# Cutting the attention scores of a hybrid layer into products of 64 by 64

## The chip, the cores and the metric

The kernel runs on one core of a Trainium2 chip. The metric is the device time of one execution in microseconds; lower is better. Times of a run are given as a median; a profile is one execution in which every instruction is recorded. The engines are TensorE (PE; its weight loads, LDWEIGHTS, have a row of their own, PEld), VectorE (DVE), ScalarE (ACT), GpSimd (POOL) and SyncE (SP), which here only issues transfers.

## The reference

Two blocks are computed one after the other on 512 tokens of width 2048 in float32. The first is one hybrid layer: a dilated banded attention of 16 heads of 64 features (three window and dilation settings, joined by a softmax over their log denominators), a gated linear recurrence of 8 heads, an output projection and a gate. The second is two layers, each with a retention of 6 heads, a differential attention of 4 heads (each with two score maps of 64 features) and a gated recurrence. Cut to what matters here:

```python
# first block: 16 heads, E = 64
q = rope_partial(heads(aq, 16), pos) * (64 ** -0.5)
k = rope_partial(heads(ak, 16), pos)
s = einsum('bdhnqe,bdhnke->bdhnqk', qb, kb)        # scores: contraction over 64 features
s = where(valid, s, NEG)                           # banded, dilated windows
pe = exp(s - max(s)); o = einsum(pe, vb) / sum(pe)

# second block, per layer: 4 heads x 2 maps, DQ = 64, causal
s = einsum('bqhcd,bkhcd->bhcqk', qb, k)            # blocks of 128 queries
p = softmax(where(kpos <= qpos, s, -inf))
w = p[:, :, 0] - lam * p[:, :, 1]
o = einsum('bhqk,bkhe->bqhe', w, v)
```

The rest of both blocks is projections with 2048 inputs, norms, gates, the recurrences and the output projections.

## The kernel before, in words

The kernel is written engine by engine: each engine has its own program, and semaphores order them. A wait stands in an engine's queue, and all behind it on this engine waits too. Most of TensorE's work is the projections. A tile of 128 output features is 16 blocks of 128 inputs; both operands are split into a high and a low float32r part, so a block is three matmuls of 128 by 128 weights on 512 tokens (`quarter`, L325). A quarter is 4 blocks, 12 matmuls, and `step` runs 4 tiles of 4 quarters, p = 0 to 15. ScalarE copies the high part of the weights (`high`, L710), GpSimd subtracts to get the low part (L262), both paced by `w_free`, which each quarter raises.

After quarter p, `step` runs the attention or recurrence work that belongs to this p, for heads whose projections ended a step earlier. For the first attention (`att_work`) a step takes a pair of heads, 8 pairs in all. Queries and keys of head 0 lie on partitions 0 to 63, those of head 1 on 64 to 127. `att_scores` (L468 to L475) makes the scores of one block of 128 queries against 512 keys for both heads, as one float32 matmul each, weights of 64 rows by 128 queries; a float32 matmul is two instructions in the trace. Head 0 goes to PSUM bank SC[0], head 1 to SC[1]. Blocks 0 to 3 stand at p = 0, 4, 8, 12. Ahead of each product stands a wait for `sm_done`: VectorE has read the scores that the bank held before (L1434, which also finds the row maximum). ScalarE then takes the exponential, VectorE scales and transposes, and `att_values` (L487, 32 by 64 weights) runs for the pair before at p = 0, right behind block 0's scores. Pair 0 is a step of its own, pairs 1 to 6 are a loop. The last pair has no tiles of its own to run with: `step(None, ...)` puts the blocks at p = 0, 2, 6, 10 (`LAST_PAIR`), with the first output projection tiles (`pair_step`, L358) between, and its values at p = 15.

The second attention (`dif_work`) is built alike: `dif_scores` (L551 to L558) for block a multiplies only the first 128 (a + 1) keys, because it is causal, at p = 0, 4, 8, 12 of a step (`GROUPED`), with waits for `dsm_done` (VectorE's read, L1523). Two layers have 4 heads each, all inside steps with tiles. Around its scores stand transposes (L389, L576) and values (L567) with weights of 128 by 128. The retention steps hold a gate product (L547) whose weights are 128 rows by 32 or 64 columns on 512 tokens.

The order on each engine is written out by hand; no planner moves anything.

Of the kernel before, what the change touches and what calls it, by code (L numbers as in the profile page):

```python
# [31 lines left out]
P = 128  # L32
# [8 lines left out]
PRIMED = 1  # L41
# [41 lines left out]
def lru_features(s):  # L83

    if s < X_JOIN:
# [8 lines left out]
GROUPED = dict(scores={0: 0, 4: 1, 8: 2, 12: 3}, softmax={1: 0, 5: 1, 9: 2, 13: 3}, turn={4: 0, 8: 1, 12: 2},  # L94
               values={8: 0, 12: 1}, turn_late={0: 3}, values_late={0: 2, 4: 3}, last=4, back=6, out=5, dif_out=6, v_copy=4)

ATT_POINTS = dict(scores={0: 0, 4: 1, 8: 2, 12: 3}, softmax={1: 0, 5: 1, 9: 2, 13: 3})
LAST_PAIR = dict(scores={0: 0, 2: 1, 6: 2, 10: 3}, softmax={1: 0, 4: 1, 8: 2, 12: 3})
# [28 lines left out]
def build(nc, wt, xT, pT, pos1, pos2, par1, par2, dlam, gw, cst, idn, masks, bias, dec, cmask, out):  # L127
    ctx = ExitStack()
    with ctx:  # L129
# [5 lines left out]
        def sem(name):  # L135
            if name not in sems:
                sems[name] = ctx.enter_context(nc.semaphore(name))
            return sems[name]
# [28 lines left out]
        SC = [ctx.enter_context(nc.psum_tensor(f"scores{i}", [P, S], F32)) for i in range(2)]  # L167
# [4 lines left out]
        def row(r, n=1):  # L172
            return W[:, r, :] if n == 1 else W[:, r:r + n, :]
# [22 lines left out]
        QT, KTR, VTA, QN, KN, RW, TM = 22, 23, 24, 25, 26, 27, 28  # L196
# [112 lines left out]
        def _(pe):  # L309
            def quarter(t, q, gen=None, spare=None, behind=2):  # L310

                bank = Z[t.odd] if spare is None else spare
                if q == 0 and spare is None:
                    if t.c in (T_HGG, T_HGG + 1) and not t.terms:
                        pe.wait_ge(sem("e_out"), 16)
                    else:
                        pe.wait_ge(sem("z_free"), t.times(1, 1 - T_HGG - behind))
                pe.wait_ge(sem("l_ready"), t.times(4, q + 1))  # L320
                for k in range(4 * q, 4 * q + 4):
                    if gen is not None:
                        pe.wait_ge(sem("u_ready"), gen * 16 + k + 1)
                    for n, (w, u) in enumerate(((WH, UH), (WH, UL), (WL, UH))):
                        mm = pe.matmul(bank[:], w[:, k, :], u[:, k, :], start=(k == 0 and n == 0),  # L325
                                       stop=(k == KT - 1 and n == 2))
                mm.then_inc(sem("w_free"), 1)
# [137 lines left out]
                if p == 14:  # L465
                    turn_v(row(HTMP), (sem("ho_scaled"), j + 1), "ho_turned", TP[1])

            def att_scores(j, a):  # L468

                for hd in range(2):  # L470
                    u = 2 * a + hd
                    pe.wait_ge(sem("sm_done"), PRIMED + j * 8 + max(u - 1, 0))
                    o = 64 * hd
                    pe.matmul(SC[hd][:], row(QT)[o:o + 64, a * P:(a + 1) * P], row(KTR)[o:o + 64, :],
                              start=True, stop=True).then_inc(sem("s_done"), 1)  # L475

            def att_values(j):

                pe.wait_ge(sem("vx_ready"), j * 16 + 16)
                pe.wait_ge(sem("p_ready"), PRIMED + j * 8 + 8)  # L480
                pe.wait_ge(sem("att_done"), PRIMED + j)
                for kb in range(16):
                    k = slice(32 * kb, 32 * kb + 32)
                    for g in range(4):
                        rows = slice(32 * g, 32 * g + 32)
                        for hd in range(2):
                            mm = pe.matmul(ATT_BANKS[g][64 * hd:64 * hd + 64, 0:P].rearrange("p (a t) -> p a t", a=4),  # L487
                                           VX[rows, hd, kb, :], W[rows, PTB + 4 * hd:PTB + 4 * hd + 4, k],
                                           start=(kb == 0), stop=(kb == 15))
                mm.then_inc(sem("av_done"), 1)  # L490

            def att_work(j, p, late=None, at=ATT_POINTS):

                if p == 0:
                    pe.wait_ge(sem("qt_ready"), j + 1)
                if p in at["scores"]:
                    att_scores(j, at["scores"][p])
                if late is not None and p == 0:
                    att_values(late)
                if p == 15 and at is LAST_PAIR:  # L500
                    att_values(j)
# [49 lines left out]
            def dif_scores(j, a):  # L551

                for hd in range(2):
                    u = 2 * a + hd
                    pe.wait_ge(sem("dsm_done"), PRIMED + j * 8 + max(u - 1, 0))
                    o, w = 64 * hd, (a + 1) * P
                    pe.matmul(SC[hd][:, 0:w], row(QT)[o:o + 64, a * P:(a + 1) * P], row(KTR)[o:o + 64, 0:w],
                              start=True, stop=True).then_inc(sem("ds_done"), 1)  # L558

            def dif_values(j, a):  # L560

# [21 lines left out]
            def dif_work(j, p, late=None):  # L583

                at = GROUPED
                if p == 0:
                    turn_v(row(VTA), (sem("dqt_ready"), j + 1), "dv_turned", VB)
                if p in at["scores"]:
                    dif_scores(j, at["scores"][p])
                if late is not None and p in at["values_late"]:  # L590
                    dif_values(late, at["values_late"][p])
                if p in at["values"]:
                    dif_values(j, at["values"][p])
                if late is not None and p in at["turn_late"]:
                    dif_turn(late, at["turn_late"][p])
                if p in at["turn"]:
                    dif_turn(j, at["turn"][p])
                if late is not None and p == at["back"]:
                    dif_turn_back(late)

            WORK = {"hg": hg_work, "att": att_work, "ret": ret_work, "dif": dif_work}

            def step(t, work=None, j=None, between={}, behind=(2, 2, 2, 2), **kw):

                for p in range(16):
                    s, q = divmod(p, 4)
                    if t is not None:
                        quarter(t.plus(s), q, behind=behind[s])
                    if work is not None:
                        WORK[work](j, p, **kw)  # L610
                    if p in between:
                        between[p]()

            pe.wait_ge(sem("p_split"), 2)
            for m in range(KT):
                t, n = divmod(m, 8)
# [4 lines left out]
                for k in range(2):  # L621
                    for i, (w, u) in enumerate(((WH, PH), (WH, PL), (WL, PH))):
                        mm = pe.matmul(Z[m % 2][:], w[:, 2 * n + k, :], u[:, k, :], start=(k == 0 and i == 0),
                                       stop=(k == 1 and i == 2))
                mm.then_inc(sem("w_free") if n % 2 else sem("e_even"), 1)

            for m in range(8):
                for q in range(4):
                    quarter(Tile(T_HGG + m), q, 0 if m == 0 else None, SPARE.get(m), 4 if m in (4, 5) else 2)
                if m == 2:  # L630
                    pe.wait_ge(sem("consts"), 16)
                    pe.wait_ge(sem("ones_set"), 1)
                    sum_rows(row(ACC), OB, (sem("sq_used"), PRIMED + 16), "ss_done")
            step(Tile(T_HG))
            with pe.Fori(1, HG_HEADS) as i:
                step(Tile(T_HG, (4, i)), work="hg", j=i - 1)
            step(Tile(T_ATT), work="hg", j=HG_HEADS - 1)
            step(Tile(T_ATT + 4), work="att", j=0, between={7: lambda: pe.wait_ge(sem("hg_done"), PRIMED + HG_HEADS)})
            with pe.Fori(2, PAIRS) as i:
# [20 lines left out]
            for l in range(LAYERS):  # L660
# [7 lines left out]
                for h in range(1, RET_HEADS + 1):  # L668
                    if h == 1:
# [4 lines left out]
                         j=l * RET_HEADS + h - 1, b=h - 1)  # L674
# [3 lines left out]
                with pe.Fori(2, DIF_HEADS) as i:  # L678
                    step(Tile(T_L2 + R_DIF, (PER_LAYER, l), (4, i)),
                         work="dif", j=l * DIF_HEADS + i - 1, late=l * DIF_HEADS + i - 2)  # L680
# [1354 lines left out]
```

## Time and profile before

| what | value |
|---|---|
| median of 3 runs | 3036.71 us (3035.82 to 3039.58) |
| the profiled execution | 3036.43 us, its span 3034.6 us |
| TensorE busy | 2955.4 us, 97% |
| VectorE, GpSimd, ScalarE busy | 1649.8, 1315.0, 1284.9 us |
| granted TensorE clock, mean | 0.991 |

The span runs from the first to the last instruction. An engine's busy time counts an instant once, however many of its instructions overlap. Matmuls overlap their neighbours in the record, so the distance between starts tells more of their cost than their durations.

### The profile page before, as it was taken

What the parts mean: (1) busy time and instruction counts of PE and PEld (TensorE: products, weight loads), DVE (VectorE), ACT (ScalarE), POOL (GpSimd) and SP (SyncE); (2) the same over time, 40 slices, a digit from 0 to 9 for tenths busy, and PEclk for the clock granted to TensorE, in tenths of its full rate; (3) what the DMA queues carried; (4) which work ended last, traced back from release to release, by engine and by line L of the source; (5) the groups of instructions that cost most, each with busy time, mean ns of one, the idle gap of its engine ahead of it and who ended that gap; (6) DMA issues with size and microseconds to landing.
All of it is one profiled execution on the core that took longest, in us unless ns stands there. A gap on an engine that the chain in (4) does not pass through costs nothing.

```text
span 3034.6 us, 48369 instructions
## 1 busy us (share of the span) xinstructions
PE 2955.4 (97%) x17162; PEld 2385.6 (79%) x17162; DVE 1649.8 (54%) x2349; ACT 1284.9 (42%) x2468; POOL 1315.0 (43%) x1002
## 2 busy tenths in 40 slices
PE   8999999999999999989999999999999999999997
PEld 6888888877777787767887878788778878787886
DVE  5367666655656315657565664561275656654412
ACT  6545444354556333443333333453343333344432
POOL 4444444443433343553444444344444444444444
PEclk9999999999999999999999999999999999999999
DMA  6223222222222323233222222232242222222322
GB/s 238 102 90 111 83 83 76 77 84 83 78 77 80 125 97 139 90 118 125 105 87 91 87 85 82 83 142 100 104 156 88 95 87 96 84 84 80 143 97 97
DMA packets 60880, 305.72 MB, mean 101 GB/s; under 512 B 5712, under 2 KB 6096, under 8 KB 29776
## 3 DMA queue, kind: packets, MB, share of 16 engines
q1 hardware_dynamic: 38224, 259.54, 24.0%
q10 hardware_dynamic: 22528, 44.50, 4.2%
q8 instruction: 77, 1.26, 0.2%
q14 instruction: 51, 0.42, 0.0%
HBM read 285.67 MB, written 18.35 MB: 100 GB/s over the span
## 4 chain that ended last, share of the span: by engine, by line
issue 56%; POOL 32%; PE 9%; POOLq 1%; DMA 1%; ACT 1%; DVE 0%; DVEq 0%; ACTq 0%; SPq 0%
POOL w_low L262 31%; PE z L325 8%; DMA w_raw<-in_wt 1%; POOLq L261 1%; POOL next_weights L270 0%; PE scores L325 0%; PE v_bank L358 0%; PE z L358 0%; ACT u_high L722 0%; DVE mixed L1647 0%; POOLq L296 0%; DVE work L1266 0%; POOLq L284 0%; POOLq L129 0%; ACT w_high L710 0%
## 5 line engine op out<-in xcount | busy, mean ns | idle before, releaser
L262 POOL TENSOR_TENSOR w_low<-w_raw,w_high 128x512 fp32r<-128x512 f32 x932 | 1254.3, 1350 | 1700.0 <-ACT w_high L710 1692.5
L325 PE MATMUL z<-u_high,w_high 128*128 128x512 f32 x3408 | 1347.6, 395 | 2.6 <-POOL w_low L262 1.8
L325 PE MATMUL z<-u_high,w_low 128*128 128x512 f32 x3408 | 1328.4, 390 | 0.0
L325 PE MATMUL z<-u_low,w_high 128*128 128x512 f32 x3408 | 1327.0, 389 | 0.0
L710 ACT ACTIVATE w_high<-w_raw 128x512 fp32r<-128x512 f32 x928 | 578.7, 628 | 1223.0 <-PE z L325 1128.3
L325 PEld LDWEIGHTS z<-u_high,w_high 128*128 128x128 f32 x3408 | 640.1, 188 | 160.2 <-issue 23.3
L325 PEld LDWEIGHTS z<-u_high,w_low 128*128 128x128 f32 x3408 | 639.6, 188 | 136.1
L325 PEld LDWEIGHTS z<-u_low,w_high 128*128 128x128 f32 x3408 | 640.5, 188 | 127.1
L1633 DVE TENSOR_TENSOR work<-work 128x512 f32<-128x512 f32 x87 | 99.9, 1148 | 365.0 <-ACT work L947 351.7
L1260 DVE TENSOR_TENSOR work<-z,work 128x512 f32<-128x512 f32 x110 | 76.1, 692 | 122.7 <-PE z L325 101.8
L1292 DVE SCALAR_TENSOR_TENSOR work<-z,work 32x512 f32<-32x512 f32 (+1 forms) x176 | 120.9, 687 | 2.4
L735 ACT ACTIVATE work<-work 128x512 f32<-128x512 f32 x72 | 45.4, 631 | 145.4 <-DVE work L1272 92.1
L341 PE MATMUL z<-u_high,next_weights 128*128 128x512 f32 x192 | 72.1, 417 | 21.1 <-DVE u_low L1618 13.6
L722 ACT ACTIVATE values_spread<-work 32x512 f32<-32x512 f32 x128 | 80.6, 630 | 19.4 <-DVE work L1449 16.4
L1316 DVE TENSOR_TENSOR work<-o_bank,head_norm 128x512 f32<-128x512 f32 x28 | 19.4, 692 | 112.5 <-ACT head_norm L748 112.5
L1279 DVE TENSOR_TENSOR mixed<-work 128x512 f32<-128x512 f32 (+1 forms) x35 | 24.3, 694 | 85.4 <-ACT work L739 85.4
L1288 DVE SCALAR_TENSOR_TENSOR work<-z,work 128x512 f32<-128x512 f32 x56 | 38.7, 692 | 58.7 <-PE z L325 56.7
L1296 DVE TENSOR_TENSOR work<-work 128x512 f32<-128x512 f32 x56 | 65.4, 1168 | 5.2
L341 PEld LDWEIGHTS z<-u_high,next_weights 128*128 128x128 f32 x192 | 38.5, 200 | 35.5 <-issue 23.4
L1347 DVE TENSOR_TENSOR work<-work 128x512 f32<-128x512 f32 x56 | 55.0, 983 | 18.8 <-ACT work L722 10.8
L722 ACT ACTIVATE work<-work 128x512 f32<-128x512 f32 (+1 forms) x96 | 58.3, 639 | 13.9 <-DVE work L1347 9.7
L1474 DVE SCALAR_TENSOR_TENSOR work<-work 128x512 f32<-128x512 f32 x72 | 60.8, 845 | 6.0 <-issue 0.9
(281 smaller groups left out, 3243.7 us busy)
## 6 DMA issues: line engine op xcount, KB each, us to landing
w_raw<-in_wt SPq DMA_DIRECT2D x241, 1024.0 KB, 4.8
out_hT<-work ACTq DMA_DIRECT2D x8, 1024.0 KB, 8.7
work<-out_hT ACTq DMA_DIRECT2D x8, 1024.0 KB, 10.4
work<-in_xT SPq DMA_DIRECT2D x4, 1024.0 KB, 17.2
e_scratch<-work ACTq DMA_DIRECT2D x1, 4096.0 KB, 16.7
work<-in_xT ACTq DMA_DIRECT2D x4, 1024.0 KB, 10.9
work<-in_dec ACTq DMA_DIRECT2D x12, 256.0 KB, 2.7
work<-rope_tables ACTq DMA_DIRECT2D x10, 256.0 KB, 2.8
```

The source lines that it names most:

```text
L262: pool.tensor_tensor(WL[:, 4 * q:4 * q + 4, :], RAW[:, t.odd, 512 * q:512 * q + 512].rearrange("p (k c) -> p k c", k=4), WH[:, 4 * q:4 * q ...
L325: mm = pe.matmul(bank[:], w[:, k, :], u[:, k, :], start=(k == 0 and n == 0), stop=(k == KT - 1 and n == 2))
L341: mm = pe.matmul(bank[:], w[x], u[:, k, :], start=(k == 0 and n == 0), stop=(k == KT - 1 and n == 2))
L710: act.activation(WH[:, 4 * q:4 * q + 4, :], RAW[:, n.odd, 512 * q:512 * q + 512].rearrange("p (k c) -> p k c", k=4), ACT.Copy).then_inc(se ...
L722: i = act.activation(dst, src, ACT.Copy, **kw)
L735: act.activation(row(r), row(r), ACT.Exp, scale=-1.0)
L1260: v.tensor_tensor(dst, (Z[t.odd] if bank is None else bank)[:], row(RSTD), ALU.mult).then_inc(sem("z_free"), 1)
L1292: i = v.scalar_tensor_tensor(out=row(TM)[o:o + half], in0=z[x:x + half, :], scalar=-scale if first else scale, in1=row(sin)[o:o + half], o ...
L1296: v.tensor_tensor(row(dst), row(dst), row(TM), ALU.add)
L1347: i = v.tensor_tensor(x, x, y, ALU.mult)
L1474: v.scalar_tensor_tensor(out=R_, in0=R_, scalar=-1.0 / f, in1=TB, op0=ALU.add, op1=ALU.mult)
L1633: i = v.tensor_tensor(row(ACC), row(ACC), row(SQ0 + s), ALU.add)
```

## The change

Both score helpers now cut each head's product of 64 rows by 128 queries into two of 64 by 64: the first 64 queries go to partitions 0 to 63 of the bank, the others to 64 to 127, against the same keys. In `att_scores` a new argument `whole` keeps head 0 as one product of 64 by 128 and cuts head 1 only; it is true at p = 0 and in the last pair. The waits between the heads are gone. Where `whole` is true one wait stands ahead of both heads; elsewhere it stands ahead of the projection quarter that precedes the scores. Each wait now asks for both heads' reads of the block before. Each head still raises its semaphore once.

```diff
-            def att_scores(j, a):
-
+            def att_scores(j, a, whole):
+
+                if whole:
+                    pe.wait_ge(sem("sm_done"), PRIMED + j * 8 + 2 * a)
                 for hd in range(2):
-                    u = 2 * a + hd
-                    pe.wait_ge(sem("sm_done"), PRIMED + j * 8 + max(u - 1, 0))
-                    o = 64 * hd
-                    pe.matmul(SC[hd][:], row(QT)[o:o + 64, a * P:(a + 1) * P], row(KTR)[o:o + 64, :],
-                              start=True, stop=True).then_inc(sem("s_done"), 1)
+                    o, w = 64 * hd, P if whole and hd == 0 else 64
+                    for x in range(0, P, w):
+                        mm = pe.matmul(SC[hd][x:x + w, :], row(QT)[o:o + 64, a * P + x:a * P + x + w], row(KTR)[o:o + 64, :],
+                                       start=True, stop=True)
+                    mm.then_inc(sem("s_done"), 1)
...
-                    att_scores(j, at["scores"][p])
+                    att_scores(j, at["scores"][p], p == 0 or at is LAST_PAIR)
...
             def dif_scores(j, a):
                 for hd in range(2):
-                    u = 2 * a + hd
-                    pe.wait_ge(sem("dsm_done"), PRIMED + j * 8 + max(u - 1, 0))
-                    o, w = 64 * hd, (a + 1) * P
-                    pe.matmul(SC[hd][:, 0:w], row(QT)[o:o + 64, a * P:(a + 1) * P], row(KTR)[o:o + 64, 0:w],
-                              start=True, stop=True).then_inc(sem("ds_done"), 1)
+                    o, n = 64 * hd, (a + 1) * P
+                    for x in (0, 64):
+                        mm = pe.matmul(SC[hd][x:x + 64, 0:n], row(QT)[o:o + 64, a * P + x:a * P + x + 64],
+                                       row(KTR)[o:o + 64, 0:n], start=True, stop=True)
+                    mm.then_inc(sem("ds_done"), 1)
...
                 for p in range(16):
                     s, q = divmod(p, 4)
+                    if work == "dif" and p in GROUPED["scores"]:
+                        pe.wait_ge(sem("dsm_done"), PRIMED + j * 8 + 2 * GROUPED["scores"][p])
+                    if work == "att" and t is not None and p in (4, 8, 12):
+                        pe.wait_ge(sem("sm_done"), PRIMED + j * 8 + p // 2)
                     if t is not None:
                         quarter(t.plus(s), q, behind=behind[s])
```

## Rows read from the trace of the kernel before

**Rows 1.** The page, part 1: busy us, share of the span, instructions.
```profile
PE 2955.4 (97%) x17162; PEld 2385.6 (79%) x17162; DVE 1649.8 (54%) x2349; ACT 1284.9 (42%) x2468; POOL 1315.0 (43%) x1002
```
**Rows 2.** Busy time by stretch: length, each engine, granted clock, transfers.
```profile
590.00:955.00 365.00, 363.56 (x2992) 279.90 (x2991) 206.47 (x403) 194.81 (x359) 148.96 (x115) 1.00 0.23 81
955.00:1010.00 55.00, 45.45 (x647) 34.14 (x646) 37.48 (x79) 31.73 (x63) 8.94 (x7) 0.91 0.11 39
1780.00:2000.00 220.00, 219.83 (x1039) 175.14 (x1038) 114.63 (x218) 92.77 (x215) 93.14 (x71) 1.00 0.23 82
...
962.70:964.60 1.90, 1.90 (x4) 0.47 (x4) 1.12 (x2) 0.59 (x2) 0.00 (x0) 0.50 0.00 0
```
**Rows 3.** Groups by shape: count, busy us, mean ns, idle before and its cause.
```profile
L474 PE MATMUL scores<-work 64*128 64x512 f32 x128 | 37.7, 657 | 4.8 <-DVE work L1302 4.2 <-DVE small L1434 0.6
...
L557 PE MATMUL scores<-work 64*128 64x512 f32 x32 | 9.0, 641 | 0.0
```
**Rows 4.** Timeline (start us, us) around one first-attention site, loads and matmuls.
```profile
673.70 0.19 PEld L325 LDWEIGHTS z<-u_high,w_low 128*128 128x128 f32 x1
674.24 0.30 PEld L474 LDWEIGHTS scores<-work 64*128 64x128 f32 x4 [0.35 <-issue]
...
674.24 0.70 PE L474 MATMUL scores<-work 64*128 64x512 f32 x2
...
674.77 0.60 PE L474 MATMUL scores<-work 64*128 64x512 f32 x2
...
675.29 0.19 PEld L325 LDWEIGHTS z<-u_high,w_high 128*128 128x128 f32 x1 [0.76 <-issue]
```
**Rows 5.** Timeline of weight loads at a second-attention site of 128 keys.
```profile
1833.11 0.30 PEld L557 LDWEIGHTS scores<-work 64*128 64x128 f32 x4 [0.17 <-issue]
1833.53 0.19 PEld L567 LDWEIGHTS o_bank<-work 128*128 128x128 f32 x1
```
**Rows 6.** Timeline of weight loads at two gate products of the retention.
```profile
1510.93 0.16 PEld L547 LDWEIGHTS scores<-work 128*32 128x32 f32 x8 [0.35 <-issue]
...
1512.78 0.19 PEld L325 LDWEIGHTS z<-u_high,w_high 128*128 128x128 f32 x1 [0.84 <-issue]
...
1561.12 0.20 PEld L547 LDWEIGHTS scores<-work 128*64 128x64 f32 x4 [0.35 <-issue]
1561.60 0.14 PEld L547 LDWEIGHTS scores<-work 128*64 128x64 f32 x2 [0.29 <-issue]
1562.03 0.14 PEld L547 LDWEIGHTS scores<-work 128*64 128x64 f32 x2 [0.28 <-issue]
1562.99 0.19 PEld L325 LDWEIGHTS z<-u_high,w_high 128*128 128x128 f32 x1 [0.81 <-issue]
```
**Rows 7.** Timeline where a transpose of 128 by 128 follows a quarter.
```profile
1484.76 0.39 PE L325 MATMUL z<-u_high,w_low 128*128 128x512 f32 x1
...
1484.77 0.14 PEld L513 LDWEIGHTS turned<-identity,work 128*128 128x128 f32 x1
```
**Rows 8.** Timeline of TensorE at block 0 of a pair.
```profile
698.60 1.13 PE L474 MATMUL scores<-work 64*128 64x512 f32 x4
699.66 0.34 PE L487 MATMUL turned<-work,values_spread 32*64 32x128 f32 x4
```
**Rows 9.** Timeline of TensorE and VectorE in the last pair.
```profile
962.66 2.08 PE L474 MATMUL scores<-work 64*128 64x512 f32 x4 [4.21 <-DVE work L1302]
...
970.58 0.71 DVE L1447 STREAM_TRANSPOSE work<-work 128x512 f32<-128x512 f32 x1 [0.30 <-PE v_bank L487]
...
999.03 0.34 PE L487 MATMUL turned<-work,values_spread 32*64 32x128 f32 x4 [3.93 <-issue]
```
**Rows 10.** Timeline: VectorE's last read of a block, and the next scores.
```profile
928.82 0.69 DVE L1434 CUSTOM_DVE_ANT_0 work<-scores,work 128x512 f32<-128x512 f32 x1
...
936.74 0.70 PE L474 MATMUL scores<-work 64*128 64x512 f32 x2
...
1791.46 0.29 DVE L1523 CUSTOM_DVE_ANT_0 work<-scores,work 128x128 f32<-128x128 f32 x1
...
1795.50 0.49 PE L557 MATMUL scores<-work 64*128 64x256 f32 x2
```

## The prediction, made before the changed kernel ran

> **What bounds the kernel now.** I read the page's busy shares first, then the busy time by stretch, then the matmul groups by shape, then single sites of the two edited helpers in the timeline. TensorE is busy for 97% of the span [rows 1]. In the stretches that hold the edited helpers it is busier still: 363.6 of 365 us where the first attention runs and 219.8 of 220 us where the second does in layer 1, both at full clock; only in the 55 us around the last pair is it idle for 9.6 us [rows 2]. The groups by shape say the same: the 128 matmuls of the first attention's scores have 4.8 us of idle time before them, 4.2 behind one wait and 0.6 behind another, and those of the second have none [rows 3]. So a microsecond added to or taken from TensorE's stream in these stretches is a microsecond of the kernel, the last pair excepted. Other engines don't enter.
>
> **What one site costs now.** A site is the products of both heads for one block of 128 queries: 4 matmul instructions, since each f32 product is two. The first attention has 128 of 512 columns, so 32 sites; the second has 32 of each of four widths, so 32 sites too (the widest in [rows 3]). Within a site the heads already run side by side: two instructions start at 674.24, the other two at 674.77, and the projection's weights load at 675.29 [rows 4]. So a site is two phases, not four, and some 1.06 us from its own weight load to the next one (674.24 to 675.29; 1.06 at the site of 698.60 [rows 8]). With 128 columns it is 0.42 (1833.11 to 1833.53 [rows 5]): 384 columns less in each of two phases are worth 0.64 us, so 512 columns stream in 0.427 us and 128 in 0.107, and about 0.20 us stand around the streaming at either width.
>
> The array is full in both phases: 2 heads x 64 rows, 128 output rows. Cutting each product into two of 64 by 64 gives four products on four quarters of the array, again in two phases of the same length. **Nothing is taken from the streaming.** What can change is what stands around it.
>
> **The split sites.** The diff splits both heads where `whole` is false: 7 pairs x 3 blocks = 21 sites in the first attention and all 2 x 4 x 4 = 32 in the second, 53 in all. No row shows 64x64 on four quarters. The nearest is a gate product of 128 rows by 64 weight columns [rows 6]: two quarters, four phases of 512 columns, 1.87 us from 1561.12 to 1562.99. Two phases less, 2 x 0.427, is 1.02 us, against 1.06 with 128 weight columns: 0.04 us less, because only 64 columns are loaded before streaming begins. Its first phase says it too, 0.48 us (1561.12 to 1561.60) against 0.53 (674.24 to 674.77). From the other side, with four narrow products side by side, 128x32, it is 1.85 for four phases (1510.93 to 1512.78 [rows 6]), so four products at once cost no more. Bounds: 0 per site (twice as many instructions to issue eat the shorter load) and 0.06 (the narrow form, 1.06 - 1.00). I take 0.04, by the row of the same width: 53 x 0.04 = 2.1 us saved, bounds 0 and 3.2.
> The Trainium skill (TensorE: Matmul & The Clock Gate, LDWEIGHTS) prices a weight load by its columns over 1.2 GHz, whatever its rows, so 64 fewer are an estimate of 0.053 us a site and 2.8 us in all, within these bounds.
>
> **The mixed sites.** Where `whole` is true head 0 stays 64 by 128 and head 1 becomes two of 64 by 64: block 0 of 7 pairs, and all 4 blocks of the last pair, 11 sites. Here two cuts of the array meet inside one site. What does the trace show when the cut changes? With the same cut the weights of the next product load while the current one streams, even across a wait and another line: L513's load starts at 1484.77 under the projection's matmul of 1484.76 [rows 7]. When the cut changes the load is held back: before the scores it starts at 674.24, 0.54 us after the one before it and with 0.35 us of idle time, and after them at 675.29, when both phases are out [rows 4]. The change of rows alone does it (128x128 to 64x128, [rows 4]) and the change of columns alone too (128x128 to 128x64, idle 0.35 before the load [rows 6]). So TensorE empties before it goes on in another cut. In none of these rows are the two products on separate parts of the array, so the trace doesn't show that head 1's rows 64 to 127 must wait for head 0's rows 0 to 63. I take it that they do: the load is held even where a spare weight buffer is plainly free in the same-cut case, so what is checked seems to be the cut, not the place.
> The Trainium skill (TensorEngine Tiling (Array Packing), Key Properties) says that changing the mode, and not just the tile, drains the engine; by it the sum is the one below, and by the bare rows, which show only overlapping places, the first rival stays open.
>
> Then head 0 takes its 1.06 us and head 1 comes after it with another 1.02 (the 64-column site above): +1.02 us a site. For the 7 sites at block 0 that is 7 x 1.02 = 7.1 us, all on the path, since the next work, the late values at 699.66, starts 1.06 us after the scores of 698.60 [rows 8]. In the last pair block 0 runs after a wait of 4.21 us at a granted clock of 0.50 [rows 2, 9]; by that clock its 1.02 would be about 1.9 (streaming doubled, 2 x 0.853, and 0.2 around it). It is passed on: VectorE waits for the values that follow (0.30 us at 970.58 [rows 9]) and is then the engine that the pair's end hangs on. The other three sites of that pair add 3 x 1.02 to TensorE, but it stands still for 3.93 us before the last values at 999.03, where the softmax is late [rows 9]; they are absorbed. Sum: +7.1 + 1.9 = +9.0 us. Bounds: 0 (heads overlap as now) and 7.1 + 1.9 + 3.1 = 12.1 (nothing absorbed).
>
> **The moved waits.** The wait before block a now stands ahead of a quarter of 12 matmuls, 2.73 us (12.18 us from one site to the next, less 1.26 for the site and the held load, over four), and asks for both heads' reads of block a - 1 at once. Behind it on TensorE are the quarter and its release of weight buffers to ScalarE. The reads are done long before in the first attention: the tightest ends at 929.5, the quarter starts at about 933.9 (936.74 less 2.73 and the 0.09 before the load). In the second the tightest is block 0 of each layer's first head: read done at 1791.8, quarter at about 1792.7, so 0.9 us in hand [rows 10]. Cost 0, and at most the lateness beyond 0.9 us at two places; if VectorE came 1 us later there, 0.2 us in all. In the last pair the wait for both heads delays head 0 of block 3 from 986.33 to about 986.95, before the same 3.93 us of slack. Removing the wait between the heads frees nothing: they start together now.
>
> **Sum.** 3036.43 us for the profiled execution (span 3034.6) + 9.0 - 2.1 = 3043.3. That execution is 0.3 us below the median of 3036.71; I say 3043.4.
>
> **Rivals.**
> 1. *The mixed sites overlap as before.* Head 1's quarters are free while head 0 streams. For it: two heads do run in one phase now [rows 4]. Against it: the held loads. Then only the split sites count: 3036.4 - 2.1 = 3034.3. The Trainium skill (TensorE: Matmul & The Clock Gate, Part 3) has weight loads overlap running matmuls exactly when the row group differs, as it does here; that would give this rival.
> 2. *The 64-column halves don't run side by side* with two row halves in use. Each split site then takes twice its streaming: 21 x 0.85 = 17.9, and in the second attention 8 x (0.21 + 0.43 + 0.64 + 0.85) = 17.0; the mixed sites' second halves another 7 x 0.85 + 1.7 = 7.7. With the sum above, 3043.3 + 42.6 = 3086. Slower whatever the mixed sites do. Against it: two products of 128x64 and four of 128x32 do share a phase [rows 6], and four of 32x64 start together in the values [rows 8].
> 3. *The hoisted wait lets the scores' weights load under the quarter.* If the 0.20 us around a site were the wait's doing, 53 x 0.20 = 10.6 us would go: 3035 with the drained mixed sites, 3026 without them. Against it: L513 has a wait ahead of it and loses nothing, and the projection's load after the scores is held too [rows 4, 7].
> 4. *A later wait in the projection*, by the 0.9 us margin: under 1 us, no case of its own.
>
> **How the numbers follow.** The forecast 0.62, rival 1 0.27, rival 2 0.04, rival 3 0.05, anything else 0.02. The forecast's own range is 3041 to 3046: its +6.9 moves with the 1.9 of the half-clock site, the absorbed 3.1 and the 0 to 3.2 of the split sites. The range that holds 8 in 10 has to take in rival 1: 3033.2 to 3046. A run of this kernel can tell about 0.2%, 6.1 us, from no change. The forecast lies at +6.7 against the median, just beyond it: I give it 0.7 to end above. Slower: 0.62 x 0.7 + 0.04 + 0.01 = 0.48. Faster, from rival 3 and the unknown rest: 0.05. Same: 0.47.
>
> **What would show it.** In the changed profile: at a mixed site (block 0 of a pair) matmuls in four start times instead of two, about 2.1 us from the first load to the next work; at a split site eight instructions in two start times, first phase 0.48 us instead of 0.53, 1.02 in all; the same idle time before the scores' load; no new wait of TensorE for VectorE's reads; the 3.93 us before the last values shrunk to about 2.8. If the mixed sites take 1.06 us, the drain step is wrong and the kernel is no slower. If a split site of 512 columns takes 1.9 us, the side-by-side step is.

## The result and the profile after

The changed kernel takes 3043.89 us (median of 20 runs, 3041.32 to 3047.77) against 3036.42 us of the kernel before (20 runs, 3035.22 to 3039.58): ratio 1.0025, 95% interval 1.0019 to 1.0031. That is 7.5 us slower, a quarter of a per cent; 3043.4 was forecast. The profiled execution took 3046.1 us, its span is 3044.3 us, so it is one of the longer ones, and 9.7 us above the span of before.

The page after, part 1, answers to [rows 1]: TensorE's busy time is up by 10.4 us, the other engines' by 3.2 at most.

```profile
PE 2965.8 (97%) x17396; PEld 2381.4 (78%) x17396; DVE 1648.4 (54%) x2349; ACT 1288.1 (42%) x2468; POOL 1312.9 (43%) x1002
```

The timeline of weight loads and matmuls (start us, us) at a split site of the first attention, the same place as [rows 4]. The site's eight matmul instructions, two for each of its four products, start in two groups, four at 676.11 and four at 676.59; from the site's load to the projection's it is 1.02 us, and the load is held back by the same 0.35 us as before.

```profile
675.57 0.19 PEld L325 LDWEIGHTS z<-u_high,w_low 128*128 128x128 f32 x1
676.11 0.21 PEld L475 LDWEIGHTS scores<-work 64*64 64x64 f32 x8 [0.35 <-issue]
...
676.11 0.66 PE L475 MATMUL scores<-work 64*64 64x512 f32 x4
...
676.59 0.61 PE L475 MATMUL scores<-work 64*64 64x512 f32 x4
...
677.13 0.19 PEld L325 LDWEIGHTS z<-u_high,w_high 128*128 128x128 f32 x1 [0.81 <-issue]
```

The weight loads at block 0 of a pair, the same place as [rows 8]. Head 0's two loads come first; head 1's four wait 1.05 us for them, with 0.76 us in which no weight loads, and the late values start at 702.45, 2.06 us after the site instead of 1.06.

```profile
700.39 0.29 PEld L475 LDWEIGHTS scores<-work 64*128 64x128 f32 x2 [0.35 <-issue]
701.44 0.20 PEld L475 LDWEIGHTS scores<-work 64*64 64x64 f32 x4 [0.76 <-issue]
702.45 0.15 PEld L489 LDWEIGHTS turned<-work,values_spread 32*64 32x64 f32 x4 [0.81 <-issue]
```

Starts of the scores of pair 2 and block 1 after it, from TensorE's timeline: 12.14 us between split sites (12.18 before) and 17.00 after a mixed one with the late values behind it (15.96 before).

```profile
676.11 1.09 PE L475 MATMUL scores<-work 64*64 64x512 f32 x8
...
688.25 1.09 PE L475 MATMUL scores<-work 64*64 64x512 f32 x8
...
700.39 2.13 PE L475 MATMUL scores<-work 64*128 64x512 f32 x6
...
717.39 1.09 PE L475 MATMUL scores<-work 64*64 64x512 f32 x8
```

The groups by shape, answering to [rows 3]: neither attention's scores wait for a read of VectorE. The only wait left is the last pair's for its queries.

```profile
L475 PE MATMUL scores<-work 64*64 64x512 f32 x212 | 36.5, 632 | 0.0
L475 PE MATMUL scores<-work 64*128 64x512 f32 x22 | 13.3, 686 | 4.2 <-DVE work L1308 4.2
L558 PE MATMUL scores<-work 64*64 64x512 f32 x64 | 8.7, 614 | 0.0
```

In the last pair, TensorE's timeline, answering to [rows 9]. Block 0 takes 3.97 us at half clock. A projection tile then stands still for 1.78 us between two of its own matmuls, block 1 takes 3.02, and the last values follow the tile of 1009.04 directly: the 3.93 us of idle time ahead of them are gone (1.14 us of idle time now stand among the values, at 1012.99).

```profile
969.05 3.97 PE L475 MATMUL scores<-work 64*128 64x512 f32 x6 [4.21 <-DVE work L1308]
...
979.15 0.39 PE L358 MATMUL z<-u_low,w_high 128*128 128x512 f32 x1
981.32 0.39 PE L358 MATMUL z<-u_high,w_low 128*128 128x512 f32 x1 [1.78 <-issue]
981.63 3.02 PE L475 MATMUL scores<-work 64*128 64x512 f32 x6
...
1009.04 0.39 PE L358 MATMUL z<-u_high,w_low 128*128 128x512 f32 x1
1009.36 0.34 PE L489 MATMUL turned<-work,values_spread 32*64 32x128 f32 x4
```

The stretch after that stall, busy time by stretch with the granted clock third from the end: 0.73 of full speed, where this part of the last pair had 1.00 before (980 to 990 us). It is half clock (1.2 of 2.4 GHz) up to about 989.5 us and full clock from there.

```profile
983.00:995.00 12.00, 12.00 (x36) 6.92 (x33) 10.18 (x18) 6.43 (x12) 1.73 (x1) 0.73 0.00 0
982.70:989.40 6.70, 6.70 (x16) 4.07 (x16) 4.95 (x12) 2.94 (x7) 0.00 (x0) 0.50 0.00 0
989.60:995.00 5.40, 5.40 (x22) 2.97 (x21) 5.11 (x7) 3.53 (x6) 1.73 (x1) 1.00 0.00 0
```

Where the 9.7 us of the two profiles come from: from the first pair's block 0 to the last pair's it is 373.6 us (595.47 to 969.05) instead of 367.1 (595.58 to 962.66), +6.5; from there to the third output tile (1018.60, before 1008.44) 49.6 instead of 45.8, +3.8; the second attention's split sites give back about 1, and what is left, under 1 us, lies in the projections between.

### The profile page after: what moved, and what is told of

Same layout as the page of the kernel before. It is cut to its first block, busy times and chain, and to the rows that moved or that the text cites. A ratio compares the mean times of both kernels' runs of the same rounds, so it can differ in the third digit from the quotient of the medians.

```text
span 3044.3 us, 48808 instructions
## 1 busy us (share of the span) xinstructions
PE 2965.8 (97%) x17396; PEld 2381.4 (78%) x17396; DVE 1648.4 (54%) x2349; ACT 1288.1 (42%) x2468; POOL 1312.9 (43%) x1002
## 4 chain that ended last, share of the span: by engine, by line
issue 56%; POOL 32%; PE 9%; POOLq 1%; DMA 1%; ACT 1%; DVE 0%; DVEq 0%; ACTq 0%; SPq 0%
POOL w_low L262 31%; PE z L325 8%; DMA w_raw<-in_wt 1%; POOLq L261 1%; POOL next_weights L270 0%; PE scores L325 0%; PE v_bank L358 0%; PE z L358 0%; ACT u_high L728 0%; DVE mixed L1653 0%; POOLq L296 0%; DVE work L1272 0%; POOLq L284 0%; ACT w_high L716 0%; ACT next_weights L723 0%
## 5 line engine op out<-in xcount | busy, mean ns | idle before, releaser
L1322 DVE TENSOR_TENSOR work<-o_bank,head_norm 128x512 f32<-128x512 f32 x28 | 19.3, 691 | 113.2 <-ACT head_norm L754 113.2
```

## The experiments

All are edits of the changed kernel; "the cut" is the shape in which a product occupies the array. Theory D is the prediction's: a second cut inside a site drains TensorE, so head 1 follows head 0.

**1. No mixed sites.**

```diff
-                    o, w = 64 * hd, P if whole and hd == 0 else 64
+                    o, w = 64 * hd, P if whole else 64
```

> The mixed sites (block 0 of every pair and the last pair) get both heads as 64 by 128 again; all else as changed. Theory D (a second cut inside a site drains TensorE, so head 1 follows head 0): the 9 us of the mixed sites go and the 53 split sites keep their 0.04 us, 3036.4 - 2.1 = 3034.3 us, ratio to before 0.9993, sites at block 0 back to 1.06 us. Rival W (the time comes from the moved waits or from more instructions, not from the mix): stays above 3040 us.

Measured: 3034.93 us (11 runs), before 3036.76, ratio 0.9995 (0.9986 to 1.0004). With head 0 and head 1 in one cut everything that the change cost is gone, though its waits, its split sites and most of its added instructions are still there. Rival W falls. Sites at block 0 are 1.06 us again (15.96 us to the next). That it is faster than before isn't shown by the times, whose interval holds 1.

**2. All sites of the first attention mixed.**

```diff
-                    o, w = 64 * hd, P if whole and hd == 0 else 64
+                    o, w = 64 * hd, P if hd == 0 else 64
```

> All 32 sites of the first attention are mixed, head 0 as 64 by 128 and head 1 as two of 64 by 64. Theory D: the 21 other sites each lose the 0.04 us and pay 1.02 more, 21 x 1.06 = 22.3 us over the changed kernel's 3043.9, so 3066.2 us, and the distance between sites goes from 12.14 to 13.20 us. Rival S (only block 0, with the late values behind it, is slow when mixed): no more than the changed kernel plus 1 us, 3045.

Measured: 3063.15 us (5 runs), ratio 1.0086 (1.0072 to 1.0100). The weight loads of a block 1, with a projection quarter behind it and not the late values, show the same wait for head 0:

```profile
609.05 0.29 PEld L475 LDWEIGHTS scores<-work 64*128 64x128 f32 x2 [0.35 <-issue]
610.10 0.20 PEld L475 LDWEIGHTS scores<-work 64*64 64x64 f32 x4 [0.76 <-issue]
611.11 0.19 PEld L325 LDWEIGHTS z<-u_high,w_high 128*128 128x128 f32 x1 [0.81 <-issue]
```

The distance between sites is 13.16 to 13.17 us. That is 1.02 more than split (12.14) and 0.98 more than uncut (12.18), so 21 x 1.025 = 21.5 us against the changed kernel, where 22.3 were expected; 19.3 were measured. The rest fits the last pair, which in this profile lacks the stall of 1.78 us and takes 47.0 us instead of 49.6. Rival S (only block 0) falls by 18 us. The price of a mixed site over the kernel before is 0.98 us where a projection follows it.

**3. The waits alone.**

```diff
-                    o, w = 64 * hd, P if whole and hd == 0 else 64
+                    o, w = 64 * hd, P
...
-                    for x in (0, 64):
-                        mm = pe.matmul(SC[hd][x:x + 64, 0:n], row(QT)[o:o + 64, a * P + x:a * P + x + 64],
-                                       row(KTR)[o:o + 64, 0:n], start=True, stop=True)
+                    mm = pe.matmul(SC[hd][:, 0:n], row(QT)[o:o + 64, a * P:(a + 1) * P],
+                                   row(KTR)[o:o + 64, 0:n], start=True, stop=True)
```

> Only the waits are moved as in the change; every product is 64 by 128 as before. Theory D and the prediction's step on waits: 3036.4 us, within 0.3 us of before. Rival W (a wait ahead of the quarter holds up the projection, or lets the scores' weights load under it): slower by some us, or faster by up to 10.6 us if the 0.20 us around a site were the wait's.

Measured: 3037.01 us (11 runs), before 3036.76, ratio 1.0002 (0.9993 to 1.0011); sites 12.18 us apart, as before. So the waits cost and free nothing that the sites or the times show. The part of rival 3 that lays the 0.20 us around a site at the wait's door falls too.

**4. The last pair uncut.** Its four blocks get both heads as 64 by 128, block 0 of the others stays mixed.

```diff
-                    o, w = 64 * hd, P if whole and hd == 0 else 64
+                    o, w = 64 * hd, P if both or whole and hd == 0 else 64
...
-                    att_scores(j, at["scores"][p], p == 0 or at is LAST_PAIR)
+                    att_scores(j, at["scores"][p], p == 0 or at is LAST_PAIR, at is LAST_PAIR)
```

> The last pair's four blocks get both heads as 64 by 128; block 0 of the other 7 pairs stays mixed, the rest stays split. Theory D: 7 x 1.02 - 2.1 = +5.0 us over before, 3041.4 us; the last pair's share of the changed kernel is what is left, 3043.9 - 3041.4 = 2.5 us. Rival L (the last pair, with its half clock, makes most of the 7.5 us): below 3039 us.

Measured: 3041.38 us (11 runs, 3040.75 to 3042.39), before 3036.76, ratio 1.0015 (1.0006 to 1.0024). Over experiment 1 that is 6.45 us for 7 mixed sites, 0.92 each by the times. By the profile the distance to block 1 grows by 0.99 us in pair 0 (12.18 to 13.17) and by 1.04 in the pairs with late values behind block 0 (15.96 to 17.00), with pair 1 counted alike 7.2 us in all; each median's interval is nearly 3 us wide to either side and doesn't tell 6.45 from 7.2. Rival L (most of it in the last pair) falls: 6.5 of the 9 us by which the changed kernel lies above experiment 1 are at block 0 of the seven pairs.

**5. Narrower still: four of 64 by 32 a head,** block 0 and the last pair uncut.

```diff
-                    o, w = 64 * hd, P if whole and hd == 0 else 64
+                    o, w = 64 * hd, P if whole else 32
...
-                    for x in (0, 64):
-                        mm = pe.matmul(SC[hd][x:x + 64, 0:n], row(QT)[o:o + 64, a * P + x:a * P + x + 64],
+                    w = 32
+                    for x in range(0, P, w):
+                        mm = pe.matmul(SC[hd][x:x + w, 0:n], row(QT)[o:o + 64, a * P + x:a * P + x + w],
```

> As the kernel without mixed sites (block 0 of every pair and the last pair 64 by 128), but the 53 split sites are cut into four of 64 by 32 per head instead of two of 64 by 64. Theory D with the weight columns as the price before streaming: the distance between first-attention sites goes from 12.14 to 12.12 us, another 53 x 0.02 = 1.1 us, 3033.9 us. Rival I (16 matmul instructions a site cost issue time): 12.14 us or more, 3035 or above.

Measured: 3037.47 us (11 runs), before 3036.83, ratio 1.0001 (0.9992 to 1.0010). Sites are 12.14 us apart, as with 64 columns, and the site's own 1.02 us is unchanged:

```profile
674.65 0.18 PEld L475 LDWEIGHTS scores<-work 64*32 64x32 f32 x16 [0.35 <-issue]
675.67 0.19 PEld L325 LDWEIGHTS z<-u_high,w_high 128*128 128x128 f32 x1 [0.84 <-issue]
```

Rival I holds, and single instructions show how. In another profile of this kernel, at the site whose load starts at 675.81, the second group of matmuls starts 0.455 us after the load, against 0.482 with 64 columns and 0.535 with 128:

```profile
676.27 0.64 PE L475 MATMUL scores<-work 64*32 64x512 f32 x8
```

So the shorter load does save 0.027 us. But the instructions of a group start 7 ns apart, and the last of eight starts 0.50 us after the load, as does the last of four with 64 columns: the extra instructions take back what the shorter load gives.

The median is also 2.5 us above experiment 1's, and its interval against before doesn't tell it from nothing. The sites don't explain it. In that other profile the last pair, uncut in both, takes 47.8 us against experiment 1's 45.4, so the difference may lie there.

**6. Two cuts, neither of them 64 by 128.** In blocks 1 to 3 of the first attention head 0 is two of 64 by 64, head 1 four of 64 by 32.

```diff
-                    o, w = 64 * hd, P if whole and hd == 0 else 64
+                    o, w = 64 * hd, P if whole else (64, 32)[hd]
```

> No product of 64 by 128 at the 21 sites of blocks 1 to 3 of the first attention: head 0 is two of 64 by 64, head 1 four of 64 by 32; the rest as in the kernel without mixed sites. Theory D (any two cuts side by side drain): distance between sites 13.12 to 13.16 us, 21 x 1.0 = +21 us, 3056 us. Rival F (only an uncut row half, 64 by 128, can't run beside a cut one): 12.14 us, 3034.9 us.

Measured: 3056.67 us (4 runs), ratio 1.0065 (1.0049 to 1.0080). The distance is 13.10 to 13.11 us, and the weight loads of the two cuts are 1.01 us apart, though the two heads use different halves of the rows:

```profile
621.90 0.20 PEld L475 LDWEIGHTS scores<-work 64*64 64x64 f32 x4 [0.35 <-issue]
622.91 0.15 PEld L475 LDWEIGHTS scores<-work 64*32 64x32 f32 x8 [0.81 <-issue]
623.90 0.19 PEld L325 LDWEIGHTS z<-u_high,w_high 128*128 128x128 f32 x1 [0.84 <-issue]
```

So it isn't the uncut half that blocks (rival F): both pairs of cuts that were tried, 64 by 128 beside 64 by 64 and 64 by 64 beside 64 by 32, follow one another. In both the heads share the columns and differ in the rows; parts that differ in the columns alone weren't tried.

**7. The second attention mixed, the first not.** Head 0 is 64 by 128, head 1 two of 64 by 64, for 128 to 512 keys.

```diff
-                    o, w = 64 * hd, P if whole and hd == 0 else 64
+                    o, w = 64 * hd, P if whole else 64
...
-                    for x in (0, 64):
+                    w = (P, 64)[hd]
+                    for x in range(0, P, w):
```

> The 32 sites of the second attention are mixed (head 0 64 by 128, head 1 two of 64 by 64), those of the first are split or 64 by 128 but never mixed. Theory D says head 1's streaming is added, which grows with the keys: 2 phases x 0.427 x n/512 and some 0.13 around it, 0.34, 0.56, 0.77 and 0.98 us for 128 to 512 keys, 8 x 2.65 = 21.2 us, less nothing; 3034.9 + 21.2 + 1.3 (the 0.04 us lost at 32 sites are in it) = 3056 to 3057 us. Rival P (a fixed penalty of 0.98 us whenever the cut changes inside a site): 32 x 0.98 = 31.4 us, 3066 us.

Measured: 3058.46 us (4 runs), ratio 1.0072 (1.0057 to 1.0087). A site of 128 keys now takes 0.78 us (0.42 in [rows 5]), one of 512 keys 2.06:

```profile
1835.41 0.61 PEld L559 LDWEIGHTS scores<-work 64*128 64x128 f32 x6 [0.17 <-issue]
1836.19 0.30 PEld L570 LDWEIGHTS o_bank<-work 128*128 128x128 f32 x2 [0.17 <-issue]
...
1875.43 0.29 PEld L559 LDWEIGHTS scores<-work 64*128 64x128 f32 x2 [0.35 <-issue]
1876.49 0.20 PEld L559 LDWEIGHTS scores<-work 64*64 64x64 f32 x4 [0.76 <-issue]
1877.49 0.19 PEld L570 LDWEIGHTS o_bank<-work 128*128 128x128 f32 x1 [0.81 <-issue]
```

The distances between sites over those of the changed kernel grow by 0.40, 0.63, 0.83 and 1.04 us with 128, 256, 384 and 512 keys. The price is head 1's own streaming plus some 0.19 us, and no fixed penalty (rival P). 8 x 2.90 = 23.2 us; over experiment 1 it is 23.5.

**8. and 9. The changed kernel again, twice.**

> The changed kernel once more, for the last pair. In its first profile TensorE stood still for 1.78 us inside a projection tile at 979.5 us and ran at half clock afterwards. If that belongs to the change, it is there again and the time is 3043 to 3044 us; if it is chance, the second profile has the last pair some 2 us shorter, while the 7 sites at block 0 keep 13.16 us to the next one.

> The changed kernel a third time. Its first profile had 49.6 us from the last pair's block 0 to the third projection tile, its second 46.3, the kernel before 45.8. If the difference between the two is a stall that comes and goes (1.78 us inside a tile and the half clock after it), this profile lies anywhere between 46 and 50 us, the sites at block 0 of the other pairs show 13.16 us again, and the time is 3041.5 to 3044 us.

Measured: 3042.32 us (11 runs, 3041.73 to 3045.43, profiled 3042.14) and 3045.05 us (9 runs, 3041.69 to 3046.14, profiled 3046.14). Taken together with the first 20, 17 of 40 runs lie between 3041.3 and 3043.0 and 23 between 3043.3 and 3047.8, while experiment 4, whose last pair is uncut, has all 11 within 1.6 us. In the second profile the last pair takes 46.3 us, the stall inside the tile is 0.74 us, and the clock stays up:

```profile
981.12 0.39 PE L358 MATMUL z<-u_high,w_low 128*128 128x512 f32 x1 [0.74 <-issue]
981.44 0.69 PE L475 MATMUL scores<-work 64*128 64x512 f32 x1
```

The stretch of 983 to 995 us of the same profile, busy time by stretch with the granted clock third from the end:

```profile
983.00:995.00 12.00, 12.00 (x51) 8.04 (x48) 11.13 (x24) 9.65 (x18) 1.34 (x1) 1.00 0.00 0
```

In the third profile (first line) it is 50.2 us, the stall 1.98 and the clock 0.72 in the same 12 us. A fourth profile of the same kernel, whose span is 3044.2 us, has 49.3 us, a stall of 1.46 and 0.72 (second line):

```profile
983.00:995.00 12.00, 12.00 (x36) 7.04 (x35) 10.18 (x18) 6.05 (x12) 1.43 (x1) 0.72 0.00 0
983.00:995.00 12.00, 12.00 (x36) 7.02 (x34) 10.58 (x20) 6.46 (x13) 1.40 (x1) 0.72 0.01 1
```

The three profiles with spans of 3044.2 and 3044.3 us have the long stall and the low clock, that of 3040.3 us (3042.14 us in all) has neither. So 3 to 4 us of the changed kernel come and go with this one place; the sites at block 0 are the same in all four (13.17 us to the next in pair 0, 16.97 to 17.00 in pairs 2 to 6).

**10. Only the last pair mixed, and 11. only its blocks 1 to 3.**

```diff
-                    o, w = 64 * hd, P if whole and hd == 0 else 64
+                    o, w = 64 * hd, P if whole and (both or hd == 0) else 64
...
-                    att_scores(j, at["scores"][p], p == 0 or at is LAST_PAIR)
+                    att_scores(j, at["scores"][p], p == 0 or at is LAST_PAIR, at is not LAST_PAIR)   # 10
+                    att_scores(j, at["scores"][p], p == 0 or at is LAST_PAIR, p == 0)                # 11
```

> Only the last pair's four blocks are mixed; block 0 of the other pairs is 64 by 128 for both heads, the rest is split. Theory D with the prediction's sum for the last pair: 3034.9 (no mixed sites) + 1.9 = 3036.8 us. Rival L (the last pair costs what the first profile of the changed kernel shows, 3.8 us): 3038.7 us.

> Only blocks 1 to 3 of the last pair are mixed. Prediction's step (3 x 1.0 us more of TensorE, absorbed by its 3.93 us of idle time ahead of the last values): 3034.9 us, the idle time 3.9 - 3 = about 1 us or the wait before block 3 gone instead, values at the same distance from block 0. Rival N (nothing is absorbed): 3037.9 us.

Measured: 3036.00 us for 10 (11 runs, 3033.89 to 3039.57; ratio 1.0000, 0.9991 to 1.0009) and 3034.64 us for 11 (11 runs; ratio 0.9995, 0.9986 to 1.0004), before 3036.34. Blocks 1 to 3 cost nothing: the last pair takes 45.4 us from its block 0 to the third tile (962.35 to 1007.75), as in experiment 1. TensorE's waits there in 11: the 0.6 us ahead of block 3 is gone and the one ahead of the values shrinks from 3.9 to 2.7.

```profile
PE scores L475 <- DVE work L1308: 4.2, 1, 4.2
PE turned L489 <- issue: 2.7, 1, 2.7
```

With block 0 mixed too (10) it is 47.1 us, 1.7 more, and 1.1 to 1.4 us by the medians. Here the whole last pair is mixed, as in the changed kernel, and yet there is no stall inside a tile and TensorE still stands idle before the last values:

```profile
999.55 0.34 PE L489 MATMUL turned<-work,values_spread 32*64 32x128 f32 x4 [2.12 <-issue]
```

## Why the prediction was right

- **Nothing taken from streaming, four products side by side:** right. A split site's instructions start in two groups; rival 2 would have shown 1.9 us where 1.02 is.
- **Split sites, 0.04 us each:** right for 512, 384 and 256 keys (12.18 to 12.14, 13.23 to 13.19 between the sites of 256 and 384 keys). With 128 keys the site itself is 0.04 shorter (0.42 to 0.38), but the distance to the next only 0.01 (12.62 to 12.61). So 21 x 0.04 + 8 x 0.13 = 1.9 us, forecast 2.1; experiment 1 is 1.8 below before, and 11 is 1.7. At 512 keys the second group of matmuls starts 0.053 us earlier, and two more instructions a group, 7 ns each, take 0.013 of it back: that is the 0.04.
- **Mixed sites, the drain:** right, and it is what decided the sign. The forecast had taken it from rows in which the parts overlap; the changed kernel's own sites and experiments 2 and 6 show it for parts on different rows, and 7 that its price is the other head's streaming. A site at block 0 takes 1.00 us more (2.06 - 1.06), forecast 1.02. Between sites it is 0.98 to 0.99 where a projection follows (13.17 - 12.18) and 1.04 where the late values follow (17.00 - 15.96); why 0.04 more pass behind those sites is open. The seven cost 7.2, forecast 7.1; experiment 4 over 1 gives 6.45. Rival 1, in which the heads overlap as before, falls.
The Trainium skill states the drain as a rule (TensorEngine Tiling (Array Packing), Key Properties), and experiments 2, 6 and 7 agree with it; in experiment 2 it costs 0.98 us a site. The Trainium skill's other rule that was weighed, that a weight load overlaps running matmuls only when the row group differs (TensorE: Matmul & The Clock Gate, Part 3), doesn't fit: in the mixed sites the row group differs and the load starts 1.05 us late, while in [rows 7] a load on all 128 rows overlaps a matmul on the same rows.
- **The last pair, +1.9 with blocks 1 to 3 absorbed:** the mechanism is right. Block 0's site grows by 1.89 us (2.01 to 3.90 from its first load to the values', in the first profile), and experiments 10 and 11 give 1.1 to 1.7, and 0. In 10, where all four blocks are mixed, the 3.93 us of idle time shrink to 2.1, forecast 2.8. What the forecast doesn't have is the stall inside a tile: in the changed kernel it comes on top, and with the half clock after it it uses up the idle time and more. The last pair is 0.5 us longer than before in the second profile and 3.8, 4.5 and 3.5 in the others. Over experiment 4 the medians of the three series give 0.9, 2.5 and 3.7.
- **The moved waits, 0:** right (experiment 3). The scores wait for no read, and the tight 0.9 us in the second attention held.

The sum: 7.2 for the seven sites less 1.9 for the split ones leaves 2.2 of the 7.5 us for the last pair; the forecast had 7.1, 2.1 and 1.9. That the median comes within 0.5 us of 3043.4 is in part luck: a stall that the forecast doesn't have moves the last pair by 3 to 4 us from one profile to the next, and the median falls between.

No version here is shown to beat the kernel before. Experiments 1 and 11 have their medians 1.7 to 1.8 us below it, as the sites' 0.04 us say, with intervals of 0.9986 to 1.0004 that don't tell them from it. Splitting all sites alike, which would carry the 0.04 us to the other 11, wasn't tried.

## What to carry to other kernels

Count what a cut of the array does to the streaming first: where two halves already run together, quartering saves only part of a weight load, 0.04 us a site here, and a cut to 32 columns nothing more. Keep all products that are to run together in one cut, even those on separate rows; here one head in another shape put the two one after the other, at the price of its own streaming and 0.19 us. The start times of the weight loads show it at once: one group for products side by side, two groups with idle time between for a drain.

## What the runs showed that was not expected

- In all four profiles of the changed kernel straight-line code of TensorE stalls for 0.7 to 2.0 us at the same place of the last pair, between two matmuls of one tile, with nothing in the profile to release it. In the profiles of the changed kernel a packet of the instruction queue moves within 1 to 2 us of it, at the end of a weight transfer of 1 MB (TensorE's first matmul after it starts at 981.32, 981.12 and 981.68 us in the first three). That its code came late behind the weights is a guess; no experiment moved the code. Experiment 10 speaks neither for it nor against: the same packet starts 9.7 us after block 0 there (9.9 in the first profile), also at the end of such a transfer, and nothing on TensorE comes more than 0.3 us late there.
- The same kind of idle time stands at the first run of a loop body: in the loop's first pass block 0 is followed by block 1 after 17.76 us before, where later passes take 15.96; the excess is 1.8 here, 1.9 in the changed kernel, 1.5 in experiment 3, 1.4 in experiment 4 and 3.6 in experiment 1, whose profiled execution is 1.6 us above its own median. So the profiles differ by 2 us at a place where the kernels do the same, which is as much as the whole gain of the split sites.
- A stall of 1.5 to 2.0 us (three profiles), in a pair that already stood still for 4.1 to 4.2 us, was followed by a granted clock of 0.72 to 0.73 in the stretch of 983 to 995 us, one of 0.74 us (one profile) by 1.00.
- Cutting from 64 to 32 weight columns frees nothing (1.02 us a site with both): the shorter load saves 0.027 us, and four more instructions a group, 7 ns apart, take it back.
